# A two-layer GLA / RWKV-7 / MoE backbone on one core: GLA head norms taken into the next head's scan, the routing code reordered, and nine slots for the down weights

## The reference, cut to what matters

```
# layer 0, end of the GLA mixer: one norm per head over its 256 value columns
def finish(y, r):
    yn = y * lax.rsqrt(jnp.mean(y * y, axis=-1, keepdims=True) + NORM_EPS) * norm_g
    yn = yn.reshape(y.shape[:2] + (GLA_VAL,)).astype(r.dtype)
    return (yn * jax.nn.silu(r)) @ w_out

# layer 1, the experts
logits = (h @ router).astype(jnp.float32)
top_logits, top_idx = lax.top_k(logits, TOP_K)
weights = jax.nn.softmax(top_logits, axis=-1)
for e in range(N_EXPERTS):
    out = out + combine[..., e:e + 1] * swiglu(h, w_gu[e], w_d[e])
```

## Time and profile before

| | us |
|---|---|
| median of 3 runs | 2488.49 (2486.59 to 2490.86) |
| the profiled execution, its own time | 2480.1 |
| its span | 2478.3 |
| PE busy | 2267.4 (91%) |
| DVE busy | 657.1 (27%) |
| ACT busy | 454.4 (18%) |
| weight and input DMA | 502.60 MB in all |

### The profile page before, as it was taken

One profiled execution on the slowest core, in us unless ns is written; L12 is line 12 of the kernel. 1 busy time (PEld: TensorE's weight loads), 2 busy tenths in 40 slices (PEclk: granted clock), 3 DMA queues, 4 the chain that ended last, 5 costly groups with the idle time before them and its releaser, 6 DMA issues.

```text
span 2478.3 us, 43079 instructions
## 1 busy us (share of the span) xinstructions
PE 2267.4 (91%) x19363; PEld 1416.9 (57%) x19364; DVE 657.1 (27%) x1175; ACT 454.4 (18%) x771; POOL 48.5 (2%) x165
## 2 busy tenths in 40 slices
PE   6999879899999999897997997989999989999986
PEld 3474644344446877787877876433776333875332
DVE  1032450400000034776467753210000101000102
ACT  3134111200000116453424433000000000000001
POOL 0000000400000000000000000000000000000000
PEclk8999889999999999999999998999999989999998
DMA  7254101522223362102340025899998999999994
GB/s 260 85 184 164 60 1 51 191 98 68 85 68 119 138 233 94 46 4 74 126 153 4 5 80 222 330 407 407 406 359 302 407 407 407 398 321 339 407 407 196
DMA packets 181951, 502.60 MB, mean 203 GB/s; under 512 B 9571, under 2 KB 73381, under 8 KB 175621
## 3 DMA queue, kind: packets, MB, share of 16 engines
q1 hardware_dynamic: 180148, 494.27, 53.5%
q0 software_dynamic: 1616, 5.54, 0.7%
HBM read 498.72 MB, written 1.05 MB: 202 GB/s over the span
## 4 chain that ended last, share of the span: by engine, by line
PE 40%; DMA 6%; SPq 6%; DVE 4%; issue 2%; ACT 1%; DVEq 0%; ACTq 0%
PE banks L968 8%; PE banks L1224 7%; PE banks L1243 7%; PE banks L1186 7%; DMA ring_arena<-in_moe_w_gu 6%; SPq L495 4%; PE banks L735 3%; SPq L502 2%; PE banks L1197 1%; PE banks L1209 1%; PE banks L1120 1%; PE banks L1179 1%; PE banks L915 1%; DVE ring_arena L1987 1%; PE banks L928 1%
## 5 line engine op out<-in xcount | busy, mean ns | idle before, releaser
L1186 PE MATMUL banks<-ring_arena 128*64 128x448 f32 x1536 | 320.2, 567 | 46.6 <-DMA ring_arena<-in_moe_w_gu 46.6
L735 PE MATMUL banks<-ring_arena 128*128 128x256 f32 (+1 forms) x1024 | 314.9, 466 | 15.4 <-DVE ring_arena L1793 9.3
L872 PE MATMUL banks<-ring_arena 128*128 128x512 f32 x704 | 305.4, 597 | 6.4 <-ACT ring_arena L1308 6.1
L735 PEld LDWEIGHTS banks<-ring_arena 128*128 128x128 f32 x1024 | 195.5, 192 | 134.2 <-issue 102.0
L1224 PE MATMUL banks<-ring_arena 128*64 128x512 f32 (+1 forms) x896 | 251.5, 605 | 7.0 <-DVE ring_arena L2204 7.0
L1186 PEld LDWEIGHTS banks<-ring_arena 128*64 128x64 f32 x1536 | 110.4, 142 | 237.3 <-issue 220.6
L968 PE MATMUL banks<-ring_arena 64*64 64x128 f32 (+1 forms) x6144 | 203.6, 256 | 35.9 <-DVE ring_arena L1992 19.1
L872 PEld LDWEIGHTS banks<-ring_arena 128*128 128x128 f32 x704 | 134.7, 192 | 176.3 <-issue 175.2
L968 PEld LDWEIGHTS banks<-ring_arena 64*64 64x64 f32 x6144 | 191.1, 135 | 42.7 <-issue 29.2
L1224 PEld LDWEIGHTS banks<-ring_arena 128*64 128x64 f32 (+1 forms) x896 | 90.5, 149 | 153.0 <-issue 151.9
L1243 PEld LDWEIGHTS banks<-ring_arena 128*64 128x64 f32 x3584 | 171.8, 137 | 9.4 <-issue 9.2
(11 more groups left out here) (340 smaller groups left out, 2006.8 us busy)
## 6 DMA issues: line engine op xcount, KB each, us to landing
ring_arena<-in_moe_w_gu SPq DMA_DIRECT2D x256, 896.0 KB, 16.3
ring_arena<-in_moe_w_d SPq DMA_DIRECT2D x112, 1024.0 KB, 17.1
ring_arena<-in_mod_w SPq DMA_DIRECT2D x48, 1024.0 KB, 6.7
ring_arena<-in_ff_w_gu SPq DMA_DIRECT2D x22, 1024.0 KB, 5.1
ring_arena<-in_ff_w_d SPq DMA_DIRECT2D x22, 1024.0 KB, 4.9
ring_arena<-in_rw_w_rkv SPq DMA_DIRECT2D x20, 1024.0 KB, 5.3
ring_arena<-in_gla_w_in SPq DMA_DIRECT2D x12, 1024.0 KB, 5.4
ring_arena<-in_gla_w_out SPq DMA_DIRECT2D x4, 1024.0 KB, 6.4
```

The source lines that it names most:

```text
L735: ins = T.matmul(b[:, 0:width], w[:, k, j * P:j * P + P], src[:, k, :], start=(k == 0), stop=(k == KT - 1))
L872: ins = T.matmul(ps[4 * (p % 2) + 2 * ab + j][:, :], w[:, k, j * P:j * P + P], H2[:, k, :], start=(k == 0), stop=(k == KT - 1))
L1186: ins = T.matmul(ps[2 * half][slots_at(h, CH), 0:BLOCK], XG[:, 2 * kp + kk, 0:CH], w[:, kk, BLOCK * h:BLOCK * h + BLOCK], start=(kp == 0 a ...
```

## The change

1. GLA: the sums of head h-1 run on PE inside head h's scan (`head_sums`, at step 1); the reciprocal of head h-1 is cut into four pieces of 128 columns, one after each of steps 2 to 5 of head h's scan (`head_rstd`), and its scaling follows head h's scan (`head_scaled`). ACT squares a head right after copying it. Only head 3's norm is left behind the scan, and the projection's first tile waits for `fn_done` one k at a time.
2. Routing: PE transposes X before H3 is ready, then makes the logits, then transposes H3; gain rows come after the positions. DVE writes `PG` before it needs the exponential, and PE's first gather waits for `PG` alone. `GAIN_ROW` moves from `sq` to `std` and `rstd`.
3. Down ring of nine slots for the eight main items: two more slots, in H3's place and in `sqn`, filled once H3's transposes are done (`h_tm` at 4). Overflow items still use seven.

```diff
-WD_UNITS, WD_RING, WD_SLOT = FE // SEG, 7, 2 * D
+WD_UNITS, WD_RING, WD_FIXED, WD_SLOT = FE // SEG, 9, 7, 2 * D
...
+        wd_slots += [at(2048, WD_SLOT), sqn[:, :]]
...
+        def wd_slot(n, u, first):
+            return (WD_UNITS * n + u) % WD_RING if first else u % WD_FIXED
...
             gate_up(0, 0, range(GU_RING))
-            down(0, 0, range(WD_RING))
+            down(0, 0, range(WD_FIXED))
+            sp.wait_ge(S["h_tm"], 4)
+            down(0, 0, range(WD_FIXED, WD_RING))
...
+            def head_sums(h):
+
+                for vt in range(2):
+                    pe.wait_ge(S["fn_sq"], 2 * h + vt + 1)
+                    T.matmul(head_sum_bank(h)[:, :], ones[:, :], sq[:, vt * TOK:vt * TOK + TOK],
+                             start=(vt == 0), stop=(vt == 1)).then_inc(S["fn_ss"], 1)
+
             for h in range(GH):
                 if h >= 1:
                     pe.wait_ge(S["att_out"], 2 * h)
+                if h >= 2:
+                    pe.wait_ge(S["fn_std"], h - 1)
...
+                    if i == 1 and h >= 1:
+                        head_sums(h - 1)
...
-            for h in range(GH):
-                for vt in range(2):
-                    pe.wait_ge(S["fn_sq"], 2 * h + vt + 1)
-                    T.matmul(ps[h % 2][:, :], ones[:, :], sq[:, vt * TOK:vt * TOK + TOK],
-                             start=(vt == 0), stop=(vt == 1)).then_inc(S["fn_ss"], 1)
-            pe.wait_ge(S["fn_done"], KT)
-            project(first["gla_o"], Y1, TOK, 4, lambda n: stat(1, n - 2, TOK) if n >= 2 else None)
+            head_sums(GH - 1)
+            pe.wait_ge(S["fn_std"], GH - 1)
+            project(first["gla_o"], Y1, TOK, 4, lambda n: stat(1, n - 2, TOK) if n >= 2 else None,
+                    lambda k: pe.wait_ge(S["fn_done"], k + 1))
...
+            pe.wait_ge(S["post_done"], 4 * KT)
+            for q in range(4):
+                for k in range(4 * (q % 2), 4 * (q % 2) + 4):
+                    ins = T.transpose(ps[q][:, (k % 4) * P:(k % 4) * P + P],
+                                      X[:, k, SEG + q // 2 * P:SEG + q // 2 * P + P], ident[:, :])
+                ins.then_inc(S["res_t"], 1)
...
-                pe.wait_ge(S["pg"], 4 * n + 4)
+                pe.wait_ge(S["pg"], 4 * n + 2)
...
+                if first and n == 0:
+                    pe.wait_ge(S["res_out"], 4)
+                    pe.wait_ge(S["gain_out"], 2)
...
+            act.wait_ge(S["sel"], 1)
+            C.activation(EXL[:, :, :], EXL[:, :, :], ACT.Exp).then_inc(S["ex_out"], 1)
             for q in range(4):
                 t, h = q // 2, q % 2
                 act.wait_ge(S["res_t"], q + 1)
...
+            def head_rstd(h, part):
+
+                dve.wait_ge(S["fn_std"], h + 1)
+                cols = slice(P * part, P * part + P)
+                link(Vv.reciprocal(rstd[:, cols], std[:, cols]))
+
+            def head_scaled(h):
+
+                for vt in range(2):
+                    k = 2 * h + vt
+                    g = VEC["gla_norm_g"] + vt
+                    link(Vv.tensor_tensor(Y1[:, k, :], Y1[:, k, :], rstd[:, :], ALU.mult))
+                    Vv.scalar_tensor_tensor(Y1[:, k, :], Y1[:, k, :], vecs[:, g:g + 1], R[:, k, :],
+                                            ALU.mult, ALU.mult).then_inc(S["fn_done"], 1)
...
+                    if h >= 1 and 2 <= i < 6:
+                        head_rstd(h - 1, i - 2)
+                if h >= 1:
+                    head_scaled(h - 1)
+            get_rstd(GH - 1, TOK, "fn_std")
+            head_scaled(GH - 1)
...
+            gather_slots([RK[:, t, 0:1] for t in range(2)], CAPS[0])
             dve.wait_ge(S["ex_out"], 1)
...
+            scatter_slots([RK[:, t, 0:1] for t in range(2)], [CMB_EXPERT[:, t, 0:1] for t in range(2)], CAPS[0])
```

More of the change, by code:

```diff
@@ L84 @@
         + [("gu", 8 * g + 4 + kp) for kp in range(4)]] + [("wd", u) for u in GROUP_DOWN[GROUPS - 1]]
-assert GU_UNITS % GU_RING == 0 and WD_UNITS % WD_RING == 0
+assert GU_UNITS % GU_RING == 0 and WD_UNITS % WD_FIXED == 0
 def hybrid_backbone(nc, A, out):
@@ L486, in _, with gate_up @@
             gu, wd = A["moe_w_gu"][0], A["moe_w_d"][0]
-            def gate_up(e, n, units):
+            def gate_up(e, n, units, first=True):
                 for u in units:
@@ L1164, in _ @@
             ins.then_inc(S["pos"], 1)
-            pe.wait_ge(S["h_tm_out"], 4)
-            pe.wait_ge(S["res_out"], 4)
-            pe.wait_ge(S["gain_out"], 2)
+            pe.wait_ge(S["gain_diag"], 1)
+            for h in range(2):
+                pe.wait_ge(S["h_tm_out"], h + 3)
+                T.matmul(ps[6 + h][:, :], ones[:, :], GAIN_DIAG[:, 4 * h:4 * h + 4, :],
+                         start=True, stop=True).then_inc(S["gain_mm"], 1)
             def scatter(n, q, cap):
```

106 lines of the change are left out of this document (50 added, 56 removed).

## The result

| | before | after |
|---|---|---|
| median of the timed runs, us | 2487.54 (2484.55 to 2490.86, 4 runs) | 2449.87 (2446.78 to 2453.97, 4 runs) |
| the profiled execution, its own time and span | 2480.1, 2478.3 | 2452.24, 2450.5 |

The ratio is 0.9852, 95% interval 0.9832 to 0.9872: 36.8 us less (31.8 to 41.8). Forecast were 29.6 us less and 2459 us, from 2451 to 2470. The two profiled executions differ by only 27.9 us, which is the first hint that the miss lies not in the mechanisms alone.

What follows compares the result with a forecast made beforehand. Bound: a chain of PE's work to 1513 us, then the expert stream with a hole, PE in two heavy items, stream, PE tail. Savings 18.4 + 6.0 + 5.15 = 29.6 us; 2488.5 - 29.6 = 2459 us, range 2451 to 2470.

Steps and rivals of the forecast that it cites:

- carried over, 2488.5 - 29.6: Whole kernel: profiled 2480.1 us plus 8.4 to the runs' median gives 2488.5; less the summed saving, 2459 us.
- GLA norms: Tail behind the scan saves 29.2 us, added scan work costs 10.8: net 18.4 us saved, bounds 2.9 and 24.1.
- Sums: Scan: sums take 1.7 us of PE in each of heads 1 to 3, costing 5.1 us.
- Pieces: Scan: four reciprocal pieces on DVE delay each head 0.65 us, costing 2.0 us for three; bounds 0 and 12.
- Scaling: Scan: DVE's scaling ahead of the masks of heads 2 and 3 delays PE about 1.0 us, twice: 2.0 us.
- D: Scan: reciprocal pieces wholly on the path and scaling unhidden; 19 us saved in all, 2469 us; chance 0.14.
- F: Scan: clock falls at head 1 and stays at half, 47 us lost, slower than before at 2506 us; chance 0.03.
- Routing: Logits at half clock, gather at full, ACT last: item 0's gate-up starts 6.0 us sooner; bounds 0.5 and 9.
- rival C: Routing stays at half clock: gate-up 0.5 to 3.1 us sooner, 25.4 us saved in all, 2463 us; chance 0.15.
- Nine slots: Down ring: two units prefetched in the stream's hole make item 7's last gate-up units land 5.15 us sooner.
- Rival E: Item 7's end: the ring's gain is not cashed; 24.4 us saved in all, 2464 us; chance 0.06.
- Rival B: Routing and scan: PE keeps full clock while busy, logits end at 1538.2; 32 us saved, 2456 us; chance 0.12.

Runs made afterwards that it cites:

- after_third: The changed kernel, unchanged, measured a third time, against the kernel before: 2455.56 us, ratio 0.9887.
- whole: The changed kernel with each head's reciprocal taken whole (512 columns) ahead of its scaling instead of in four pieces: 2459.40 us, ratio 0.9899 to the kernel before.
- ring_alone: The kernel before with only the nine-slot down ring, its two further units issued after the router's logits: 2477.88 us, ratio 0.9983.
- gain_early: The changed kernel with gain matmuls moved behind the X transposes, and ACT's gain and X copies ahead of the H copies: 2450.11 us, 0.9874 to the kernel before.
- gla_only: The kernel before with only the GLA part (sums, reciprocal pieces, scaling in the next head's scan; projection's waits): 2460.42 us, ratio 0.9913.
- after_again: The changed kernel, word for word, measured a second time on another chip, against the kernel before: 2452.87 us, ratio 0.9878.

## Why the prediction came out as it did

**The step that failed is the one from the sum to the time and its range, "carried over, 2488.5 - 29.6".** It took a median of three runs for the level and gave the saving as if it would be measured without error; how far medians of a few runs stray had no term, and the range was made of mechanisms' bounds alone. What the runs show in its place: the kernel before had medians from 2480.7 to 2487.5 us in five sessions, single runs of it spread over 19 us and those of after over 13, and one and the same change measured 36.8, 30.3 and 28.1 us. Against the four later sessions (mean of their medians 2482.9) the level 2488.5 was 5.6 us too high; 2482.9 - 30.1 = 2452.8, inside the range, and the measured 2449.87 lies another 2.9 below that. In the first session itself the level was right to 1 us (2487.54) and the saving was 7.2 larger than forecast. A draw would explain both readings; the chip isn't excluded.

The sum 29.6 came out near the traces' 30.1, and that is in part luck: its terms were off with opposite signs (GLA 20.0 to 20.7 for 18.4, routing beside nine slots 5.3 for 6.0, ring 4.8 for 5.15), and no timing knows the saving to better than 3 us.

**GLA norms.** The tail's 29.2 us were exact: 13.55 to 13.71 us from head 3's copy to the first emptied tile in all five traces with this part. The scan is read from ACT's copies of head 0 and head 3, here in the kernel before (its head 3 stands in the earlier trace rows) and in after_third:

```profile
289.19 1.07 ACT L1378 COPY ring_arena<-banks 128x512 f32<-128x512 f32 x2 [30.59 <-PE banks L831]
```

```profile
287.48 1.07 ACT L1412 COPY ring_arena<-banks 128x512 f32<-128x512 f32 x2 [27.52 <-PE banks L866]
...
346.69 1.07 ACT L1412 COPY ring_arena<-banks 128x512 f32<-128x512 f32 x2 [10.34 <-PE banks L866]
```

It cost 7.4 us (59.21 against 51.83 before, three times 17.28) where the clock held, and 8.9 and 9.1 where it fell at head 3; I had 10.8. With the clock up, head 1 took 19.31 us and heads 2 and 3 19.95. Sums: 18.85 - 17.28 = 1.57 us a head (head 1 of whole, which has the sums and no pieces) for my 1.7. Pieces: 19.31 - 18.85 = 0.46 a head for my 0.65; the steps' room was larger than I read. Scaling: 19.95 - 19.31 = 0.64, twice, for my 1.0. Together 7.4. The clock's fall, which I charged once at 1.7 us, came in two of the three executions of after, at about 1.6. Rivals D and F are out.

**Routing.** The logits at half clock (7.0 us) and the gather at full clock (3.7) came as read in five of the six traces of the table with this part; in the sixth the clock was still down at the gain. ACT was not the last releaser: the gather was, and gate-up started 6.9 us sooner instead of 6.0. What I had no term for is gate-up's own start: before, it began at half clock and its first release came 3.28 us behind it, now 1.77. Together 8.4 us. With nine slots the hole should let 6.65 of it through (11.8 - 5.15); 5.3 to 5.9 arrived at item 5. The first execution of after came near rival C: gate-up 3.2 us sooner, against C's 0.5 to 3.1, and the re-issue 4.8.

**Nine slots.** 4.8 us for 5.15 at the end, though item 5 comes about 1 us later with nine slots than with seven where the new routing is in (598.9 and 597.9), so that the ring adds 3.5 there. Rival E is out: ring_alone has the release of item 0 and item 5 where they were (47.1 and 604.8) and the end 4.2 us sooner by time.

**The rule against the row.** The Trainium skill (TensorE: Matmul & The Clock Gate, "Part 1: The HAM clock gate") says that the monitor runs freely, so that the same kernel meets the clock's change at another place in each run. The traces agree: gain and gather of one kernel took 3.76 + 4.55 us in one execution and 1.96 + 3.68 in another. Rival B, which read the page's release by activity into the logits, is out in all of them: the logits took 6.83 to 7.00 us, PE busy throughout. The clock did come back with PE at work, only too late for the logits. This is where the forecast did right to go by the row.

What stays open: why the first measurement gave 36.8 us, a draw or the chip; where routing's 8.4 us at the re-issue become 6.3 at item 5 with seven slots; and why routing alone was timed twice at 9 us.

## What to carry to other kernels

Cut a trace at events that belong to one queue (first issue, first re-issue, an item's issue, output) and compare distances, not end times: three parts that time could only give to 3 to 6 us each came out to 1 or 2 us. Size the range of a forecast median by the spread of single runs too, and take a second execution's profile before moving anything that looked long in one. Moving work off a path that it wasn't on gains nothing (gain_early), and the gap that it leaves may cost the clock of what follows.

## What the runs showed of the hardware

- The two executions of the kernel before stand within 0.3 us of each other at 2421 us and part by 7 in the last 60: 1.7 us by the clock in the last down stretch and 4.7 behind the first output issue. The three of after are 6.1 us apart at SP's first unit already (1492.6 to 1498.7), with a granted clock of 0.80 to 0.93 from 1440 to 1490 us. The clock doesn't fall in the same place each time: with the same code and the same waits in the scan, head 3 started at full clock in gla_only and after_third and at half in after, after_again and gain_early.
- After an idle of 5.3 us PE stayed at 1.2 GHz (granted clock 0.50) through 7.0 us of products of 8 columns and beyond, with PE busy: full clock was back 10 us behind the first of them in after_again (0.50 up to 1522, 0.75 from 1522 to 1523) and 18 us in after (0.50 up to 1531, 0.98 from 1531 to 1532).
- The expert stream runs at 407 GB/s on one core in the slices in which SP finds free slots (slices 27 to 29 and 32 to 34 of the changed kernel's page), and at 312 to 351 in those where PE holds the slots longer, items 2 and 5.
- A reciprocal on DVE took 0.95, 1.75 and 3.35 us for 128x128, 128x256 and 128x512, so 0.80 us for each further 128 columns; an elementwise product of two 128x512 tiles took 0.68.
